# Two transformer blocks on one core: forgetting attention normed with tokens on partitions, memory queries left raw with their norm as the exponential's scale, and outputs ahead of the next softmax

## The reference, cut to what matters

```python
def rmsnorm(x, g):
    y = xf * lax.rsqrt(jnp.mean(xf * xf, axis=-1, keepdims=True) + EPS)
    return (y * g.astype(jnp.float32)).astype(x.dtype)

fq = rmsnorm(heads(fq, FOX_HEADS), fox_qnorm[l])          # forgetting attention
fk = rmsnorm(heads(fk, FOX_HEADS), fox_knorm[l])
logf = jax.nn.log_sigmoid((ff + fox_fbias[l]).astype(f32))
ya = fox_attention(fq, fk, heads(fv, FOX_HEADS), logf)

def memory_cross_attention(h, m, w_q, w_kv, q_g, k_g, w_o):
    q = rmsnorm(heads(h @ w_q, MEM_HEADS), q_g)
    k, v = jnp.split(m @ w_kv, 2, axis=-1)
    k = rmsnorm(heads(k, MEM_HEADS), k_g)
    s = jnp.einsum("bqhd,bkhd->bhqk", q, k) * MEM_DIM ** -0.5
    p = jax.nn.softmax(s, axis=-1)
    o = jnp.einsum("bhqk,bkhd->bqhd", p, v)
    return o @ w_o
```

## Time and profile before

| | us |
|---|---|
| median of three runs | 1174.89 |
| the profiled execution | 1173.07 |
| its span, first to last instruction | 1171.4 |
| TensorE busy (matmul) | 1145.2 |
| VectorE busy | 812.5 |
| ScalarE busy | 622.3 |
| GpSimd busy | 82.1 |

### The profile page before, as it was taken

One profiled execution on the slowest core, in us unless ns is written; L12 is line 12 of the kernel. 1 busy time (PEld: TensorE's weight loads), 2 busy tenths in 40 slices (PEclk: granted clock), 3 DMA queues, 4 the chain that ended last, 5 costly groups with the idle time before them and its releaser, 6 DMA issues.

```text
span 1171.4 us, 16802 instructions
## 1 busy us (share of the span) xinstructions
PE 1145.2 (98%) x6765; PEld 999.7 (85%) x6765; DVE 812.5 (69%) x881; ACT 622.3 (53%) x801; POOL 82.1 (7%) x114
## 2 busy tenths in 40 slices
PE   8999999999999999999999999999999998999997
PEld 7978898889987799999888888888777887888886
DVE  6897658756878568787548777547776747777743
ACT  7666446436478466565345444436456547444432
POOL 7101100200000000000000000002700000000000
PEclk9999999999999999999999999999999999999999
DMA  8654333334665354655655655555633534665560
GB/s 259 190 158 147 99 106 110 109 108 156 220 198 181 108 163 156 204 169 191 216 179 181 210 179 186 200 195 177 201 116 127 180 108 127 194 202 182 179 214 36
DMA packets 144420, 193.95 MB, mean 166 GB/s; under 512 B 6168, under 2 KB 121240, under 8 KB 144344
## 3 DMA queue, kind: packets, MB, share of 16 engines
q1 hardware_dynamic: 143144, 188.43, 49.7%
q0 software_dynamic: 1200, 4.46, 1.1%
HBM read 191.82 MB, written 1.05 MB: 165 GB/s over the span
## 4 chain that ended last, share of the span: by engine, by line
PE 83%; DVE 10%; ACT 4%; issue 2%; DMA 0%; DVEq 0%; ACTq 0%
PE banks L1328 23%; PE banks L1362 19%; PE banks L1310 13%; PE banks L1331 11%; DVE wlo L1920 4%; PE banks L1347 3%; PE banks L1338 2%; PE banks L1589 1%; PE banks L1477 1%; ACT whi L1649 1%; PE banks L1464 1%; PE banks L1376 1%; PE banks L1547 1%; DMA x_tok<-in_x 0%; DVE x_tok L2193 0%
## 5 line engine op out<-in xcount | busy, mean ns | idle before, releaser
L1920 DVE TENSOR_TENSOR wlo<-raw,whi 128x2048 fp32r<-128x2048 f32 (+1 forms) x178 | 406.5, 2291 | 122.5 <-ACT whi L1649 122.4
L1649 ACT ACTIVATE whi<-raw 128x2048 fp32r<-128x2048 f32 (+1 forms) x179 | 340.1, 1903 | 248.3 <-PE banks L1331 146.0
L1328 PE MATMUL banks<-xhl,whi 128*128 128x512 f32 x1232 | 396.2, 403 | 2.7 <-DVE y5l L2248 1.8
L1331 PEld LDWEIGHTS banks<-xhl,wlo 128*128 128x128 f32 x1232 | 231.4, 188 | 54.6
L1331 PE MATMUL banks<-xhl,wlo 128*128 128x256 f32 x1232 | 242.6, 278 | 0.0
L1328 PEld LDWEIGHTS banks<-xhl,whi 128*128 128x128 f32 x1232 | 188.9, 189 | 10.3 <-issue 5.6
L1310 PE MATMUL banks<-xhl,whi 128*128 128x256 f32 x912 | 165.5, 284 | 1.3 <-DVE xhl L1947 0.7
L1310 PEld LDWEIGHTS banks<-xhl,whi 128*128 128x128 f32 x912 | 142.0, 192 | 2.1 <-DVE xhl L1947 1.1
L1310 PE MATMUL banks<-xhl,wlo 128*128 128x256 f32 x456 | 129.0, 283 | 0.0
L1362 PE MATMUL banks<-whi,hh 128*128 128x512 f32 x264 | 102.9, 390 | 0.0
L1362 PE MATMUL banks<-wlo,hh 128*128 128x512 f32 x264 | 102.7, 389 | 0.0
(11 more groups left out here) (368 smaller groups left out, 1531.9 us busy)
## 6 DMA issues: line engine op xcount, KB each, us to landing
raw<-in_w_in SPq DMA_DIRECT2D x40, 1024.0 KB, 5.3
raw<-in_w_up SPq DMA_DIRECT2D x22, 1024.0 KB, 5.8
raw<-in_ffn_w_gate SPq DMA_DIRECT2D x22, 1024.0 KB, 5.3
raw<-in_ffn_w_up SPq DMA_DIRECT2D x22, 1024.0 KB, 5.3
raw<-in_ffn_w_down SPq DMA_DIRECT2D x22, 1024.0 KB, 5.0
raw<-in_w_down SPq DMA_DIRECT2D x11, 1024.0 KB, 5.6
raw<-in_w_out SPq DMA_DIRECT2D x8, 1024.0 KB, 5.2
raw<-in_xa_wkv SPq DMA_DIRECT2D x8, 1024.0 KB, 5.7
```

The source lines that it names most:

```text
L1328: pe.matmul(bank(b[m]), wh[:, k, m * P:(m + 1) * P], both[:, k, :, :].rearrange("p a t -> p (a t)"), start=(k == 0), stop=(k == KD - 1), s ...
L1331: ins = pe.matmul(bank(b[m])[:, 0:T], wl[:, k, m * P:(m + 1) * P], Xh[:, k, :], start=False, stop=(k == KD - 1), skip_group_check=True)
L1649: act.activation(columns(whi, c, part), columns(raw, c, part), ACT.Copy).then_inc(act_done, 1)
L1920: dve.tensor_tensor(columns(wlo, c, part), columns(raw, c, part), columns(whi, c, part), ALU.subtract).then_inc(dve_done, 1)
```

## The change: what it does

1. Forgetting attention: fq and fk are made by V chunks (two halves each, as fv), so that they have tokens on partitions. Per matrix ScalarE squares the two token tiles (`tn_sq`), VectorE sums within each head (`tn_red`), ScalarE takes the root of eight values per partition (`tn_r`), VectorE multiplies (`tn_mul`), TensorE transposes eight blocks (`tn_t`), and ScalarE writes them back with the gain as its scale (`tn_e`). The four `hn` jobs go.
2. Memory attention: the queries stay raw. Their squares (`q_sq`) are summed by products with a single column of ones (`q_sum`), which gives one number per token and head with tokens on partitions; `q_r` makes its root, which becomes the exponential's scale and multiplies the maximum. Both gains and the factor sit in the key norm (`msc`). The two `mq` jobs of the norm go, and mk0 and mk1 are two chains with banks and buffers of their own.
3. The values of the memory go to banks 2, 3; the two following xk chunks exchange banks; head 1's scores no longer wait for the values' copy.
4. The norm mem_g_2 is scaled after both mq chunks, its transposes are four pieces at hooks of their own, on a ring of two banks, and the `drain` between mq and mv goes.
5. In the memory heads the output product and its copies stand ahead of the next head's maximum and exponential, and its division is a link of its own.

```diff
-        for i in range(2):
-            wide(win, c0 + 256 * i, "x", "add", to=what, i=i)
+        vals(win, c0, "x", "vcopy", to=what)
...
-    vals("w_mkv", 512, "m1", "vcopy", (6, 7), to="mv")
+    vals("w_mkv", 512, "m1", "vcopy", (2, 3), to="mv")
...
-    xa_k(0, (2, 3))
-    xa_k(1, (0, 1))
+    xa_k(0, (0, 1))
+    xa_k(1, (2, 3))
...
+    def token_norm(m):
+
+        return [[("act", "tn_sq", m), ("dve", "tn_red", m), ("act", "tn_r", m)], [("dve", "tn_mul", m)],
+                [("pe", "tn_t", m), ("act", "tn_e", m)]]
...
-            if nxt is not None:
+            if nxt is not None and kind in ("mem",):
+                turn_.insert(1, ("pe", "sc", kind, nxt))
+                out_ += [("dve", "sm", kind, nxt), ("act", "ex", kind, nxt)]
+            elif nxt is not None:
...
+            if nxt is not None and kind in ("mem",):
+                links += [[("dve", "pn", kind, nxt)]]
...
-    b += hn("fq0", "fq1", "fk0", "fk1")
+    b += token_norm("fq") + token_norm("fk")
...
-    side.append(hn("mk0", "mk1"))
+    side.append(hn("mk0"))
+    side.append(hn("mk1"))
     pl.add("pool", "mem2_load")
     mm(c)
-    norm_scale("mem_g_2")
+    side.append([[("act", "q_sq", 0)]])
     mm(c + 1)
     c += 2
-    drain()
+    norm_scale("mem_g_2")
     stage[0] = "mem"
-    side.append(hn("mq0", "mq1"))
-    turn_m2 = [[lambda: norm_turn("mem_g_2", 0, "m2")]]
+    turn_m2 = [[lambda j=j: norm_turn("mem_g_2", 0, "m2", js=(j,))] for j in range(4)]
     side.append(turn_m2)
...
-    for lane in range(2):
-        side.append(heads_of("mem", [lane, lane + 2]))
+    lanes = [heads_of("mem", [lane, lane + 2]) for lane in range(2)]
+    lanes[0][0][1:1] = [("pe", "q_sum", 0), ("pe", "q_sum", 1), ("act", "q_r")]
+    side.append([[("act", "q_sq", 1)]] + lanes[0])
+    side.append(lanes[1])
...
+            def tn_t(m):
+                pe.wait_ge(dve_done, at("tn_mul", m))
+                if m == "fq":
+                    pe.wait_ge(dve_done, at("hn_mul", "gk1"))
...
+                for t in range(NT):
+                    for h in range(NH):
+                        ins = pe.transpose(bank(6 + t)[:, h * P:(h + 1) * P], src[:, t, h * P:(h + 1) * P], ident[:, :])
...
+            def q_sum(i):
...
+                for n in range(4):
+                    o = 512 * i + n * P
+                    ins = pe.matmul(bank(5)[:, 4 * i + n:4 * i + n + 1], xv_[:, 0, o:o + P], ones[:, 0:1], start=True, stop=True)
...
-                    if h == 1:
-                        pe.wait_ge(act_done, at("copy", chunk_of("mv", None)))
...
+            def tn_sq(m):
...
+                act.activation(S1[:, :], TO[m][:, 0, :], ACT.Square)
+                act.activation(PT1[:, :], TO[m][:, 1, :], ACT.Square).then_inc(act_done, 1)
...
-                                         scale=f, accum_out=rs[:, t:t + 1])
+                                         scale=q_root[:, 2 * h + t:2 * h + t + 1] if kind == "mem" else f, accum_out=rs[:, t:t + 1])
...
+                dve.scalar_tensor_tensor(msc, pcolumn("mq_norm"), float(HD) ** -0.5, pcolumn("mk_norm"), ALU.mult, ALU.mult)
...
+            def tn_red(m):
...
+                dve.tensor_reduce(token_root[:, 0:4], per_head(S1[:, :]), AX_X, ALU.add)
+                dve.tensor_reduce(token_root[:, 4:8], per_head(PT1[:, :]), AX_X, ALU.add).then_inc(dve_done, 1)
...
+            def tn_mul(m):
...
+                dve.tensor_tensor(v, v, token_root.unsqueeze(2).to_broadcast([P, NT * NH, P]), ALU.mult).then_inc(dve_done, 1)
```

More of the change, by code:

```diff
@@ L36, with turn_ring @@
 PAIRS = ((0, 1), (2, 3), (4, 5), (6, 7))
+def turn_ring(name):
+    return 2 if name == "mem_g_2" else 4
 def turns(name):
@@ L82 @@
          ("pc", "moba"): 0.5, ("pv", "moba"): 0.65, ("oc", "moba"): 0.3, ("ol", "moba"): 0.44,
+         "q_sq": 0.66, "q_sum": 0.9, "q_r": 0.45,
          ("sc", "mem"): 0.86, ("sm", "mem"): 0.9, ("ex", "mem"): 1.1, ("pn", "mem"): 0.95, ("pt", "mem"): 0.88,
@@ L279, in input_of @@
         if name == "sc" and args == ["mem", 1]:
-            return pl.ended.get(("copy", max(c for c, ch in enumerate(chunks) if ch.get("to") == "mv")), 1e9)
-        if name == "sc" and args[0] == "mem" or name == "pt" and args == ["mem", 0]:
-            return pl.ended.get(("hn_mul", "mq1" if name == "pt" else f"mq{args[1] // 2}"), 1e9)
+            return max(pl.ended.get(("q_r",), 1e9), pl.ended.get(("hn_mul", "mk1"), 1e9))
+        if name == "sc" and args == ["mem", 0]:
+            return max(pl.ended.get(("hn_mul", "mk0"), 1e9), pl.ended.get(("q_sq", 1), 1e9))
+        if name == "tn_t":
+            return pl.ended.get(("hn_mul", "gk1"), 1e9)
         if name == "rows0p":
@@ L570, in fill_and_turn, with norm_turn @@
             pl.add("dve", "add", c)
-    def norm_turn(name, base, into="x", beside={}):
+    def norm_turn(name, base, into="x", beside={}, js=None):
         pl.norm_base[name] = base
         for j, ks in enumerate(turns(name)):
-            pl.take(("nt", name, j), (base + j % 4,), ("nl", name, ks[-1]))
+            if js is not None and j not in js:
+                continue
+            pl.take(("nt", name, j), (base + j % turn_ring(name),), ("nl", name, ks[-1]))
             pl.add("pe", "nt", name, j)
@@ L1758, in hn_r, with tn_r, tn_e, q_sq @@
                 act.activation(flat(rr[:]), flat(rr[:]), ACT.Exp, scale=-0.5).then_inc(act_done, 1)
+            def tn_sq(m):
+                act.wait_ge(act_done, at("copy", chunk_of(m, None)))
+                if m == "fk":
+                    act.wait_ge(dve_done, at("tn_red", "fq"))
+                act.activation(S1[:, :], TO[m][:, 0, :], ACT.Square)
+                act.activation(PT1[:, :], TO[m][:, 1, :], ACT.Square).then_inc(act_done, 1)
+            def tn_r(m):
+                act.wait_ge(dve_done, at("tn_red", m))
+                link(act.activation(token_root, token_root, ACT.Ln, bias=eps, scale=1.0 / HD))
+                act.activation(token_root, token_root, ACT.Exp, scale=-0.5).then_inc(act_done, 1)
+            def tn_e(m):
+                act.wait_ge(pe_done, at("tn_t", m))
+                act.wait_ge(dve_done, at("params_c"))
+                gain = gsc if m == "fq" else pcolumn("fox_knorm")
+                for t in range(NT):
+                    ins = act.activation((fq_ if m == "fq" else fk_)[:, :, t * P:(t + 1) * P], per_head(bank(6 + t)), ACT.Copy, scale=gain)
+                ins.then_inc(act_done, 1)
+            def q_sq(i):
+                act.wait_ge(dve_done, at("add", chunk_of("mq", i)))
+                act.activation(mat(xv_[:, 0, 512 * i:512 * i + 512]), mq_[:, 2 * i:2 * i + 2, :], ACT.Square).then_inc(act_done, 1)
+            def q_r():
+                act.wait_ge(pe_done, at("q_sum", 1))
+                link(act.activation(q_root, bank(5)[:, 0:8], ACT.Ln, bias=eps, scale=1.0 / HD))
+                act.activation(q_root, q_root, ACT.Exp, scale=-0.5).then_inc(act_done, 1)
             def g_exp(t):
@@ L2103, in sm @@
                     ins = dve.tensor_reduce(nm, bank(b).rearrange("p (t k) -> p t k", t=NT), AX_X, ALU.max, negate=True)
-                if FACTOR[kind] != 1.0:
+                if kind == "mem":
+                    link(ins)
+                    dve.wait_ge(act_done, at("q_r"))
+                    ins = dve.tensor_tensor(nm, nm, q_root[:, 2 * h:2 * h + 2], ALU.mult)
+                elif FACTOR[kind] != 1.0:
                     link(ins)
```

49 lines of the change are left out of this document (33 added, 16 removed).

## The result

The changed kernel takes 1179.65 us (median of 5 runs, 1179.48 to 1181.1) where the kernel before takes 1174.81 in the same session: a ratio of 1.0045, 95% interval 1.003 to 1.006. It is slower, and I had forecast it faster, at 1171.5 us, in a range up to 1173.5.

What follows compares the result with a forecast made beforehand. TensorE, busy 1145.2 of 1171.4 us, was taken to bound the kernel through its work and waits. Forgetting stage -2.2, memory stage -1.0 and splits -0.2 gave -3.4 us: median 1171.5 us, range 1169.1 to 1173.5.

Steps and rivals of the forecast that it cites:

- Forgetting stage, work: TensorE work for fq and fk: V chunks save 0.45 us, dropped sums 3.5, added transposes cost 1.74; sum -2.2 us.
- Forgetting stage, waits: TensorE's waits around the new token norm: no change, between 0.5 us less and 1.0 us more.
- Memory stage, work: Two mq sums go (-1.74 us), two q_sum steps come (+1.78), split mem_g_2 transposes add 0.1.
- Rival four: Memory queries' q_sum: one-column products go at the issue rate, not the loading rate; 1170.1 us, chance 0.05.
- Memory stage, waits: Old TensorE waits before w_mo and for mq's second sum go (-3.1 us); new ones of 2.0 us come.
- (d): Memory stage: head 1's transposes wait for its normalising on VectorE, behind four low halves and a difference; 1.2 us.
- (a): Memory stage: the key norm's first sum, one hook earlier, waits for its square on ScalarE; 0.6 us.
- (b): Memory stage: the first piece of mem_g_2's transposes waits for the norm's scaling, moved behind both mq chunks; 0.2 us.
- (c): Memory stage: the fourth transpose piece, with only two banks, waits for the second piece's low halves; 0.5 us.
- The 0.2 us that I gave to mk's and mq's splits: Memory stage: mk's and mq's splits no longer stand behind norm_scale, 0.2 us saved.
- The slower one: Memory stage's two-bank ring: third and fourth transpose pieces each wait behind two full splits, 2 x 4.2 us; 1177.9 us, chance 0.05.
- Five: The heads' new order makes fox or memory links later and the stage gains no work; 1174.9 us, chance 0.05.

Runs made afterwards that it cites:

- e9: The changed kernel with its own order, but at two places VectorE's z_lk step exchanged with the delta rule's copy l_xc behind it: 1178.92 us, ratio 1.0036 to before.
- e13: The changed kernel with all steps shared with before placed as before has them in the forgetting and delta rule stage: 1170.67 us, ratio 0.9968 to before.
- e4: The changed kernel with the planner's early-placing allowances in the first stages cut from 0.5 and 0.6 us to 0.2 and 0.3: 1171.38 us, ratio 0.9974 to before.
- e3: The changed kernel with the first forgetting scores held back to about where the kernel before has them: 1181.34 us, ratio 1.0054 to before.
- e5: The kernel before with only the planner's early-placing allowances cut from 0.5 and 0.6 us to 0.2 and 0.3: 1180.0 us, ratio 1.0049 to before.
- e1: The kernel before with only the forgetting part of the change (point 1), the memory stage as before: 1182.69 us, ratio 1.0069 to before.
- e11: The kernel before with both early-placing allowances lowered by 0.1 us, to 0.4 and 0.5: 1178.78 us, ratio 1.0034 to before.
- e14: The kernel before with all steps shared with the changed kernel placed as that has them in the forgetting and delta rule stage: 1185.01 us, ratio 1.0091 to before.
- e15: The kernel before with both early-placing allowances raised by 0.1 us, to 0.6 and 0.7: 1179.7 us, ratio 1.005 to before.

## Why the prediction was wrong, step by step

**Forgetting stage, work: right.** Forecast -2.2, measured -2.07 and -2.34, or -2.0 in both orders if the stages' waits are taken off (223.78 to 221.80, 226.16 to 224.19). One tn_t shows by itself (TensorE in time, answers to the earlier trace rows): eight transposes hold it 93.20 - 92.41 = 0.79 us, forecast 0.87.

```profile
92.41 1.04 PE L1460 MATMUL banks<-ident,fq_ 128*128 128x128 f32 x8
93.20 0.70 PE L1354 MATMUL banks<-xhl,whi 128*128 128x512 f32 x2
```

**Forgetting stage, waits: this step failed.** The term stood at 0, at most 1.0 us more; measured were 7.8 us more of waits (9.6 against 1.8), and with what goes beside them the new order costs 10.3 us. I took "no change, the middle, since the same planner with the same allowance places the new links", with 1.0 us above as the bound, and wrote that next "nothing" is late and that the delta rule chain was one "which the change leaves alone". The change leaves its steps alone, not their places. The planner compares clocks that it adds up itself, and a norm that loads these clocks differently moves every later link of every chain. The new order happened to have 9.6 us of waits. My bound counted only the new links, each half a microsecond early; it should have counted the links of the delta rule's 14 levels and of the four stick-breaking heads as well. A few nudged orders of the kernel before would have given the bound: the orders tried (five with the old steps of the norm, eleven with the new ones) have waits of 1.7 to 9.9 us, and 1.8 us in before was the low end of this, not its middle. The waits alone explain 8.0 of the 10.4 us of the order (9.6 and 9.9 against 1.7 and 1.8). About 0.15 us that each wait hides under a modelled end, as shown above for one, would be another 1.4 for nine more waits (an estimate); the last microsecond stays open.

**Memory stage, work: right.** The two `q_sum` steps stand in one piece (TensorE in time, answers to the earlier trace rows):

```profile
376.83 1.84 PE L1469 MATMUL banks<-ones,xv_ 128*128 128x1 f32 x16
378.54 0.63 PE L1402 MATMUL banks<-ident,xs 128*128 128x128 f32 x4
```

16 records in 1.71 us are 0.107 each and 0.855 a step, forecast 0.89. Rival four (the issue rate) is out. The Trainium skill (TensorE: Matmul & The Clock Gate, section LDWEIGHTS) gives 107 ns and with that the estimate of 0.85: the trace agrees.

**Memory stage, waits: right, and a little less than feared.** The wait before w_mo and that for mq's second sum are gone. In their place (340 to 425 us):

```profile
PE banks L1617 <- DVE S L2212: 0.9, 1, 0.9
PE banks L1447 <- ACT S L1798: 0.4, 1, 0.4
PE banks L1402 <- DVE xs L2011: 0.2, 1, 0.2
```

These are (d), (a) and (b): 0.9, 0.4 and 0.2 us, forecast 1.2, 0.6 and 0.2; (c), forecast 0.5, is a wait of 0.10 us at 383.35, too short for this view. The stage is 1.26 us shorter, forecast 1.0 and 0.2. The 0.2 us that I gave to mk's and mq's splits can't be told apart in this; no run shows it. Here I had laid out the few steps; in the forgetting stage I had laid out none.

**The rivals.** None was this. The slower one looked for its mechanism in the memory stage's bank ring, where the only wait is of 0.1 us. Five was about fewer gains, not about new waits. The range ended at 1173.5 because every case in it assumed that waits in untouched code stay.

**Open.** Which property of an order makes its waits isn't settled. Neither the density of the delta rule chain (D) nor a single queue (e9) decides. Whether the order of before is a lucky draw or was kept for being fast the runs can't say; they say only that four nudged or foreign orders of its steps are all slower, by 4 to 11 us, and that the changed steps have at least three orders under 1171.5 us.

## What to carry to other kernels

Where a program writes down the order of all engines by simulated clocks, an edit to one chain changes the place of every step behind it; price it as a new draw of the whole stage's waits, and bound this from both kernels' plans or by nudging the planner of the kernel before, which costs one run. A change of a few microseconds is judged only with the order held fixed (as in e13) or over several orders on both sides. An experiment that points the right way (e4) needs its control on the old kernel before it is taken as a cause.

## What else the runs showed of the hardware

**VectorE stands still beside GpSimd.** The multiplication by -1 of 128x384 elements in `z_lk` takes 0.36 us, and 1.31 when it meets GpSimd's mask product. GpSimd in the changed kernel, the mask beside the rows at 196.23:

```profile
195.77 2.92 POOL L1233 TENSOR_TENSOR gMs<-gM,lev 128x512 f32<-128x512 f32 x2 [8.53 <-DVE gY L2151]
```

In e9, where it comes after the masks, the same operation is short again:

```profile
198.56 0.36 DVE L2239 TENSOR_SCALAR PT<-PT 128x384 f32<-128x384 f32 x1
198.96 0.49 DVE L2241 TENSOR_TENSOR PT<-PT,sbm 128x128 f32<-128x128 f32 x2
```

The 18 traces hold this multiplication 72 times: 51 times without GpSimd beside it, always 0.36 us, and 21 times with it, always 1.31 to 1.34. The operations of L2234 and L2236 lose 0.95 and 0.98 us, together more than the 1.22 us that `l_x` then waits. The Trainium skill (SBUF — State Buffer, section SBUF: two separate sides) says that VectorE in a two-port mode, or with two SBUF inputs against a GpSimd operation that reads SBUF, and GpSimd share a port pair as an exclusive lock; the trace agrees: GpSimd's two products end at 197.32 and 198.69, and the two slow VectorE operations at 197.54 and 198.84, just behind them. It is no cause of the loss by itself. The kernel before has the same collision (1.33 us at 196.66) without a wait of TensorE, because nothing urgent stands behind it, and e3 and e9, in which all four of these multiplications are short, still have waits of 9.6 and 8.7 us.

**The granted clock.** In a few short stretches the clock falls to its lower level of 1.2 GHz, mostly for some 3.4 us, sometimes for 6.8. In the changed kernel (columns as in the earlier trace rows, the clock is the third number from the right):

```profile
850.00:856.00 6.00, 6.00 (x21) 4.27 (x21) 5.08 (x9) 1.48 (x5) 0.27 (x1) 0.72 0.74 247
987.00:994.00 7.00, 6.99 (x35) 6.71 (x35) 4.45 (x14) 5.95 (x13) 0.00 (x0) 0.53 0.17 61
```

TensorE is busy throughout in both, but it had waited just before: 1.51 us until 848.81 and 1.59 us until 985.01. That holds for every such stretch: the 18 traces have 33 between the first 20 and the last 20 us or so, and each begins between 0.2 us before and 2.0 us after the end of a TensorE wait of 1.46 to 3.47 us. The reverse doesn't hold: of 64 waits of 1.45 us or more 31 are followed by none. So a wait of TensorE can cost more than its own length. The trace of before has only one such place (0.77 from 974 to 981 us). One more stretch of 3.4 us at half the clock costs up to 1.7 us, which covers the 1.1 us by which the rest of the kernel is longer; executions of the changed kernel differ by as much (spans of 1177.7 to 1179.4). Executions at the same mean clock are the fairer comparison: at 0.998 the spans are 1171.0 to 1171.5 us for before and 1177.7 and 1177.9 for the changed kernel, 6.2 to 6.9 apart, and the two stages give 8.2 - 1.3 = 6.9.

**The old wait before w_mo could bring the lower clock.** With the new steps the stage takes 61.21 to 61.28 us in all eleven kernels that have the whole change, whatever their order before it. With the old steps it takes 62.49 us in before, 62.48 in e5 and 62.23 in e1, but 64.04 to 64.09 in e11, e14 and e15. These three have the same waits as before there (0.9 and 2.2 us), but in them 3.4 us at half the clock follow the wait for `y2l` before w_mo. In e11, the stretch and TensorE in time, with products of 512 columns 0.43 us apart and then 0.24:

```profile
402.00:406.00 4.00, 3.52 (x9) 2.85 (x10) 0.23 (x1) 1.51 (x1) 0.00 (x0) 0.57 0.00 0
```

```profile
402.49 0.77 PE L1362 MATMUL banks<-whi,y2h 128*128 128x512 f32 x1 [2.21 <-DVE y2l L2127]
403.05 0.63 PE L1362 MATMUL banks<-wlo,y2h 128*128 128x512 f32 x1
403.48 0.63 PE L1362 MATMUL banks<-whi,y2l 128*128 128x512 f32 x1
...
406.59 0.40 PE L1362 MATMUL banks<-wlo,y2h 128*128 128x512 f32 x1
406.83 0.40 PE L1362 MATMUL banks<-whi,y2l 128*128 128x512 f32 x1
```

So part of the distance of these three profiled executions from before, 1.6 us, is this and not the order. None of the twelve kernels with the new memory steps has that wait, and none has the lower clock in this stage.
